# g_final broadcast by TensorE at each tile's end, and two V rows per tile given to VectorE

## What is computed

```python
def peer_ffn(h, w_q, sub_keys, u_tab, v_tab):        # per block of 128 tokens
    q = (hb @ w_q).reshape(PEER_BLOCK, PEER_HEADS, 2, PEER_KEY_DIM // 2)
    ...                                               # top 16 of 128 x 128 keys for each of 8 heads
    gate = jax.nn.softmax(top_s, axis=-1).astype(hb.dtype)
    act = jax.nn.gelu(jnp.einsum('thkd,td->thk', u_tab[e], hb), approximate=False)
    return jnp.einsum('thk,thkd->td', gate * act, v_tab[e])
...
    xp = xp + peer_ffn(rmsnorm(xp, g_ffn[l]), ...)
y_prompt = rmsnorm(xp, g_final)[:, N_META:]
y_sample = rmsnorm(xs, g_final)
```

## Time and profile before

| | us |
|---|---|
| median of 3 runs | 3367.15 |
| span of the profiled execution | 3372.4 |
| TensorE busy | 2967.9 |
| VectorE busy | 2247.2 |
| ScalarE busy | 1569.5 |
| POOL busy | 1299.0 |

### The profile page before, as it was taken

The page is one execution under the profiler, slowest core; times in us unless marked ns, Lnnn a source line. Parts: engine busy times, 40 slices in busy tenths (PEclk is TensorE's granted clock), DMA queues, the critical chain, the costliest instruction groups (busy, mean ns, idle before and its releaser), DMA issues.

```text
span 3372.4 us, 34890 instructions
## 1 busy us (share of the span) xinstructions
PE 2967.9 (88%) x10654; PEld 1563.0 (46%) x10654; DVE 2247.2 (67%) x5353; ACT 1569.5 (47%) x4312; POOL 1299.0 (39%) x1097
## 2 busy tenths in 40 slices
PE   7988899988999898989898888998897988798877
PEld 5764556653445444554454333443353434353322
DVE  1268737685678647884779568866777486873854
ACT  2137334555456334643456345644563454432433
POOL 0023324344344434443434444453334443343532
PEclk8998999999999999999999999999999998899999
DMA  4279999999999999999999999999999989999998
GB/s 175 91 298 362 387 386 396 418 394 421 421 420 411 421 422 419 393 405 422 421 400 413 421 422 421 410 421 422 396 382 408 422 351 333 353 393 369 421 422 342
DMA packets 241250, 1298.74 MB, mean 385 GB/s; under 512 B 46068, under 2 KB 70804, under 8 KB 100646
## 3 DMA queue, kind: packets, MB, share of 16 engines
q0 software_dynamic: 156672, 1140.92, 82.5%
q1 hardware_dynamic: 84390, 155.59, 12.4%
HBM read 1279.41 MB, written 16.44 MB: 384 GB/s over the span
## 4 chain that ended last, share of the span: by engine, by line
PE 44%; DMA 28%; DVE 20%; ACT 4%; issue 2%; SPq 1%; POOL 0%; DVEq 0%; ACTq 0%
PE PS L1096 21%; DMA R<-in_t_uv,idx 18%; DVE R L1746 8%; PE PS L779 7%; DMA R<-in_t_uv,idxS 4%; DMA wring<-in_w_out 3%; PE PS L745 2%; PE PS L1018 2%; PE PS L860 2%; PE PS L859 2%; DVE xb L1757 2%; DMA wring<-in_w_query 2%; PE PS L1045 2%; DVE SC L1712 1%; DVE SC L1709 1%
## 5 line engine op out<-in xcount | busy, mean ns | idle before, releaser
L1096 PE MATMUL PS<-R,diag 128*128 128x512 f32 x3776 | 1821.4, 619 | 200.3 <-ACT diag L1378 173.6
L710 POOL DMA_INDIRECT R<-in_t_uv,idx x1024 | 1234.3, 1205 | 1949.1 <-PE PS L1096 1389.3
L1746 DVE CUSTOM_DVE_ANT_0 R<-R,hb 128x1024 f32<-128x1024 f32 x1088 | 1315.7, 1220 | 726.4 <-DMA R<-in_t_uv,idx 645.3
L1096 PEld LDWEIGHTS PS<-R,diag 128*128 128x128 f32 x3776 | 694.6, 195 | 1077.5 <-issue 635.4
L1369 ACT ACTIVATE acts<-dots 128x1 f32<-128x1 f32 x1088 | 217.2, 200 | 1103.1 <-DVE dots L1746 1100.4
L1378 ACT ACTIVATE diag<-ident,wv 128x128 f32<-128x128 f32 x880 | 353.7, 402 | 76.9 <-PE PS L1096 49.0
L779 PE MATMUL PS<-R 128*128 128x128 f32 (+2 forms) x2272 | 317.1, 295 | 38.6 <-ACT stg L1140 26.7
L779 PEld LDWEIGHTS PS<-R 128*128 128x128 f32 x2272 | 298.5, 196 | 113.1 <-issue 104.5
L1371 ACT ACTIVATE wv<-gate,acts 128x1 f32<-128x1 f32 x1024 | 301.9, 295 | 33.3
L1757 DVE SCALAR_TENSOR_TENSOR xb<-R,wv,xb 128x1024 f32<-128x1024 f32 x144 | 184.4, 1281 | 1.7 <-ACT wv L1371 1.7
L1018 PE MATMUL PS<-wring,T 128*128 128x512 f32 x256 | 133.0, 649 | 42.6 <-DMA wring<-in_w_out 42.6
(11 more groups left out here) (243 smaller groups left out, 2376.0 us busy)
## 6 DMA issues: line engine op xcount, KB each, us to landing
wring<-in_w_out SPq DMA_DIRECT2D x64, 512.0 KB, 14.0
wring<-in_w_query SPq DMA_DIRECT2D x64, 512.0 KB, 8.1
R<-in_t_win SPq DMA_DIRECT2D x38, 512.0 KB, 8.5
R<-in_t_uv,idx POOLq DMA_INDIRECT x1024, 14.0
R<-in_t_win SPq DMA_DIRECT2D x9, 1024.0 KB, 16.0
pr<-prd SPq DMA_DIRECT2D x8, 976.0 KB, 12.7
prd<-stg SPq DMA_DIRECT2D x54, 128.0 KB, 7.6
xb<-in_x_prompt SPq DMA_DIRECT2D x8, 512.0 KB, 7.9
```

The costliest lines, as they stand in the source:

```text
L710: e.indirect_dma_start(dst, None, table, bass.IndirectOffsetOnAxis(ap=index, axis=0)).then_inc(S[s], c.count(name, s, 16))
L1096: m = mm(bank(n), diag[:, NTH[s] % DR, :], pair(s)[:, D + 512 * n:D + 512 * n + 512], start=begins, stop=s == last_slot(t), skip_group_che ...
L1746: e.tensor_tensor_reduce(u, u, hb[:, tile_of(g) % 2, :], 1.0, 0.0, ALU.mult, ALU.add, dots[:, g % NW:g % NW + 1]).then_inc(dve_done, c.cou ...
```

## The change

g_final is no longer loaded per tile. Its two halves are loaded once at the start into free rows of krg (gfin_half), which becomes 1152 wide while PP becomes 1040 wide. In the turn of ysum TensorE waits for ysum and spreads g_final over the 128 partitions with two matmuls of ones (1x128) by a half (1x512) into banks 0 and 1; y then reads Y in place of gfin, after a wait for these matmuls. Since y reads the banks, the first V row that TensorE sums for the next tile waits for y, not for ysum. on_dve also gives VectorE slots 0 and 1 of tiles 2 to 8, so that TensorE's first V row there is that of slot 2, which it reaches in the turn of y. In tile 9 it is still slot 0.

```diff
--- before.py
+++ after.py
@@ -80,7 +80,7 @@
 
 
 def on_dve(s):
-    return s < P * NTILE and 3 <= s % P < 57 and s % P % 3 == 2
+    return s < P * NTILE and (3 <= s % P < 57 and s % P % 3 == 2 or s >= P and s % P < 2)
 
 
 BY_PE = [s for s in range(NSLOT) if not on_dve(s)]
@@ -208,14 +208,14 @@
         epsc = sb("epsc", [P, 2])
 
         ckvT = sb("ckvT", [P, NKEY])
-        krg = sb("krg", [P, NKEY])
+        krg = sb("krg", [P, 1152])
         ckvR = sb("ckvR", [P, (NTILE + 1) * P])
         state = sb("state", [P, 4, 64])
 
         pr = sb("pr", [P, IN_W])
         T1 = sb("T1", [P, D])
         B1 = sb("B1", [P, D])
-        PP = sb("PP", [P, 1152])
+        PP = sb("PP", [P, NKEY])
         scr = sb("scr", [P, 1152])
         ckvS = sb("ckvS", [P, KV])
         krS = sb("krS", [P, ROPE])
@@ -272,7 +272,6 @@
         mask = mask16[:].bitcast(BF16)
 
         held = wring[:, 0:2, :].rearrange("p a d -> p (a d)")
-        gfin = wring[:, 2, :]
         sst = R[:, SAUX:SAUX + 2, :].rearrange("p a (b c e) -> p (a b) c e", b=4, c=4)
         cachev = [R[:, SAUX + 2, :], R[:, SAUX + 3, :]]
         kcT = R[:, SAUX + 4, :]
@@ -282,6 +281,9 @@
         latS = R[:, SAUX + 6, 512:1024]
         pgt = stg[0:1, 0, 0:DEC_B * PAGES].bitcast(I32)
 
+        def gfin_half(n):
+            return krg[32 * n + 32:32 * n + 33, 640:1152]
+
         def gffn_half(n):
             return krg[32 * n + 32:32 * n + 33, 0:512]
 
@@ -378,7 +380,7 @@
             ["w0", "w1", "w2", "w3", "px0", "px1", "px2"] + [f"wc{i}" for i in range(NWC)] + ["ps0", "ps1", "ps2", "ps3", "pr", "prb", "pr0st",
              "xb0", "xb1",
              "trg0", "trg1", "ld_id", "early", "const", "ld_w", "kv_out", "ckvr", "y0", "y1", "st_in", "st_out", "late",
-             "pg", "cv0", "cv1", "gfin"]
+             "pg", "cv0", "cv1"]
         S = {n: ctx.enter_context(nc.semaphore(n + "_done" if n in ("dve", "act", "pe", "pool") else n)) for n in names}
         dve_done, act_done, pe_done, pool_done = S["dve"], S["act"], S["pe"], S["pool"]
 
@@ -464,6 +466,8 @@
             dma(iota[:], A["c_iota"], "const", "iota")
             for n in range(2):
                 dma(gffn_half(n), A["g_ffn"][:, 512 * n:512 * n + 512], "const", f"gffn{n}")
+            for n in range(2):
+                dma(gfin_half(n), A["g_final"].rearrange("(o n) -> o n", o=1)[:, 512 * n:512 * n + 512], "const", f"gfin{n}")
             dma(keysT[:], A["t_keys"], "const", "all")
 
             def prep(p, nj):
@@ -625,8 +629,6 @@
                     e.wait_ge(pe_done, c.at("pe", "meta su"))
                 else:
                     e.wait_ge(pe_done, c.at("pe", f"used q{t - 1}_{NCH - 1}"))
-                if m == 2 and t > 2:
-                    e.wait_ge(dve_done, c.at("dve", f"y{t - 2}"))
                 w = A["w_out" if which == "o" else "w_query"].rearrange("o k n -> (o k) n")
                 k = m % NCH
                 dma(w_buf(t, m), w[k * P:(k + 1) * P, :], f"w{m % nb}", f"{which}{t}_{k}")
@@ -660,9 +662,6 @@
                 for m in range(NCH + nb, 2 * NCH):
                     yield from p.to(1 + m - nb - NCH)
                     load_w(t, m, p)
-                yield from p.to(8)
-                e.wait_ge(pe_done, c.at("pe", f"used q{t}_6"))
-                dma(gfin, A["g_final"].partition_broadcast(P), "gfin", f"g{t}")
 
             def peer(g):
                 for t in range(1, SMP + 1):
@@ -1082,13 +1081,22 @@
                 m.then_inc(pe_done, c.count(f"sc1_{j}"))
 
             def peer(g):
+                for t in range(1, SMP + 1):
+                    if g == last_slot(t) + LAG + 1:
+                        e.wait_ge(dve_done, c.at("dve", f"ysum{t}"))
+                        if t == 1:
+                            e.wait_ge(pool_done, c.at("pool", "ones1"))
+                            e.wait_ge(S["const"], c.at("const", "all"))
+                        for n in range(2):
+                            m = mm(bank(n), ones(n), gfin_half(n), start=True, stop=True)
+                        m.then_inc(pe_done, c.count(f"gfin{t}"))
                 s = g - LAG
                 if not 0 <= s < NSLOT or on_dve(s):
                     return
                 t = tile_of(s)
-                begins = s == P * (t - 1)
+                begins = s == next(x for x in BY_PE if tile_of(x) == t)
                 if begins and t > 1:
-                    e.wait_ge(dve_done, c.at("dve", f"ysum{t - 1}"))
+                    e.wait_ge(dve_done, c.at("dve", f"y{t - 1}"))
                 if s == 0:
                     e.wait_ge(act_done, c.at("act", f"P0_{len(ITEMS[0]) - 1}"))
                 e.wait_ge(act_done, c.at("act", f"d{s}"))
@@ -1736,9 +1744,8 @@
                         e.wait_ge(act_done, c.at("act", f"ysq{t}"))
                         invert(peerv[:, 1:2])
                         settle()
-                        if t < SMP:
-                            e.wait_ge(S["gfin"], c.at("gfin", f"g{t + 1}"))
-                        stt(xb[:, t % 2, :], xb[:, t % 2, :], peerv[:, 1:2], gfin, ALU.mult, ALU.mult).then_inc(
+                        e.wait_ge(pe_done, c.at("pe", f"gfin{t}"))
+                        stt(xb[:, t % 2, :], xb[:, t % 2, :], peerv[:, 1:2], Y, ALU.mult, ALU.mult).then_inc(
                             dve_done, c.count(f"y{t}"))
                 if g < NSLOT:
                     e.wait_ge(S[f"uv{home(g)}"], c.at(f"uv{home(g)}", f"u{g}"))
```

## The result

The changed kernel takes 3395.3 us (median of 5 runs, 3383.37 to 3402.59) where the kernel before, in 5 runs beside it, takes 3368.29: a ratio of 1.0074, 95% interval 1.0051 to 1.0097. That is 17 to 33 us slower. (Every ratio here is estimated from all runs of a kernel and of before beside it, and differs a little from the quotient of the two medians, which is 1.0080 here. A ratio is turned into microseconds by before's time.) The prediction said 4 us, and its range ended at 3381. The profiled execution of after has a span of 3400.8 us, 28.4 more than before's.

What follows compares the result with a forecast made beforehand. DMA was taken to bound second halves of tiles, TensorE the stretches behind tile ends. Loads -7.4 plus 11 of 13.8 us of delay gave +3.6, say +4, on 3367.15: 3371 us, range 3358 to 3381.

Steps and rivals of the forecast that it cites:

- Loads, -7.4: Eight g_final loads go; six, in DMA-bound stretches, come off the time at 1.24 us each: -7.4 us.
- Scores end when they did: At tile ends the broadcast pair, 1.9 us warm, takes the first V row's place and the scores behind end as before.
- The moved rows: At the end of tile 3 VectorE idles 3.58 us before the masked maximum, so its two new rows (2.4 us) are hidden.
- Slots 2 and 3: Waiting for y at the ends of tiles 1, 3, 4 and 6, they end 3.1, 1.9, 4.1 and 2.7 us later: 11.8.
- The cushion at ends 2 and 5: At the ends of tiles 2 and 5, delays of 2 to 2.5 us each go into a cushion: 0.5 us together.
- End of tile 7, 1.5: Slot 2 and the scores come some 3 to 4 us later; the early refill of slot 1's pair gives 2.5 back: 1.5.
- End of tile 8, nothing: Slot 1024 waits for y, some 5 us after ysum; a cushion of 7 us takes the delay: nothing.
- Four fifths paid: Of the 13.8 us of delay at the tile ends, four fifths, 11 us, become time.
- B: VectorE reaches y later than worked out; every end pays fully at the low clock: +13 us, 3380; chance 0.26.
- C: At tile ends VectorE's moved rows don't start before y, which comes 2 us later still: 3382; chance 0.06, in B's tail.

Runs made afterwards that it cites:

- e2: Kernel before plus VectorE taking slots 0 and 1 of tiles 2 to 8 and TensorE's first V row waiting for y; g_final still loaded, no broadcast: 1.0045 of before.
- e4: The whole change, with two full matmuls (4 passes) on TensorE ahead of the broadcast pair at each tile's end: 1.0055 of before.
- e5: As e2, but at the end of tile 7 TensorE waits for ysum as before instead of y: 1.0051 of before.
- e6: The whole change, with three full matmuls into an unused bank between the scores and the wait for y at ends 1 to 6: 1.0045 of before.
- e11: The whole change, with the broadcast pair behind the scores at the ends of tiles 1 to 6, y left in place: 1.0023 of before.
- e8: As e1, but TensorE's first V row of tile 8 alone waits for y, those of tiles 2 to 7 for ysum: 1.0033 of before.
- e7: The whole change, with y one turn earlier on VectorE: 1.0005 of before.
- e10: The whole change, with y one turn earlier on VectorE and the broadcast pair behind the scores at the ends of tiles 1 to 6: 1.0009 of before.
- e12: The whole change, with the pair behind the scores except at ends 3 and 7, and y one turn earlier except at end 4: 3371.37 us, 0.9992 of before.
- e9: Kernel before without the loads of g_final and the two waits that belong to them, everything else the same: 0.9978 of before.
- e1: Kernel before with the exchange of rows alone: VectorE takes slots 0 and 1 of tiles 2 to 8; g_final still loaded, first V row waits for ysum: 1.0002.

## Why the prediction was wrong

Two steps failed above all: that the scores end when they did, and with them y at ends 3, 5 and 6, and the 1.5 us for the end of tile 7. The price is a sum of lateness at the ends. In the table of ends after's sum is 33.6 us above before's; less 7.4 for the loads that is 26, and 25 were measured. That this fits so well is in part luck: 2.3 us of it are the later cache page at end 7, and for other kernels the sum is a rough guide only. It gives 27 for e2 (15 measured), 23 for e4 (19), 21 for e5 (17), 20 for e6 (15), 16 for e11 (8), 4 for e8 (11), -5 for e7 (+2), -7 for e10 (+3), -6 for e12 (-3).

- *Loads, -7.4.* Right, size included (e9).
- *Scores end when they did.* Wrong, and the step on which most of the loss beyond the parts hangs (e11). I took the pair at 1.9 us and warm, in the first V row's place. It takes 1.13 to 2.08 us; the trace of before had it already, since the four passes of g_ffn take 1.13 us together at each of their nine places. Behind it the scores run at the low clock at ends 2, 4, 5 and 6 (e4's full pair undoes that); at end 4 this isn't so in every execution, as e6 and e7 have them at 1.12 us a pair there. At end 5 they end 10.6 us behind ysum, before 9.1. The masked maximum waits for them and y for the maximum: y starts 12.1 us behind ysum at end 5 and 14.0 at end 6, before 10.5 and 12.2. I had it unchanged at ends 3, 5 and 6, and 1.6 later at end 4, where it came 2.1 later. The moved rows themselves are hidden at ends 3, 5 and 6, as said.
- *Slots 2 and 3.* I took 4.7 us at end 3 and 5.2 at end 4, with slot 3 warm again. They took 5.40 and 6.20, at end 5 6.68. Slot 3's lateness at ends 1, 3, 4 and 6 came to 2.0, 4.1, 5.6 and 5.2 us, together 16.9 against 11.8.
- *The cushion at ends 2 and 5.* 3.7 and 5.7 us of lateness, and 0.5 forecast as paid. The place of each dot against before shows both: over the first 32 slots of tiles 3 and 6 after loses 3.7 and 5.7 us, over the rest it wins 3.7 and 4.7. A load's 1.24 us is in each rest, so 2.5 and 3.5 us came back from the cushion, and 1.2 and 2.2 us were paid, 3.4 against 0.5.
- *End of tile 7, 1.5.* The largest miss. I saw that y came late there and priced slot 2 and the scores at 3 to 4 us. That part was right: behind the cache page they came 4.1 us later, and the other 2.3 of the 6.4 us are the page itself. What was wrong is what it costs. I let the early pair of slot 1 give 2.5 us back, and nothing of that can be seen: tile 8 takes 410.5 us from its first dot to the next tile's where it took 396.8, and e8 measured 10.4 us (by its ratio over e1's; 2 to 19 by both intervals). Against the exchange alone the scores are 6.9 us late behind the page, since the exchange had brought them 2.9 us forward. Why 4 to 7 us at the scores become 11 to 15 over the tile isn't shown.
- *End of tile 8, nothing.* Right: from the first to the 33rd slot of tile 9 after loses 0.7 us.
- *Four fifths paid.* Too low, as far as one trace each can tell. Behind ends 1, 3, 4 and 6 after loses 2.1, 3.5, 4.1 and 8.5 us over the first 32 slots, together 18.2 where slot 3's lateness was 16.9. In tile 7 after's dots are 5.2 us later at slot 4, still 5.2 at slot 16, and 8.5 at slot 32.

Of the rivals B was nearest: the wait for y decides at every end but the last, and it named the sample steps' chain at tile 7. But it had the scores on time too, so even its +13 fell short. C did not occur: both moved rows start ahead of y, 2.3 and 4.6 us behind ysum at ends 1 to 7.

What stays open: the share of the clock (e4, e6), and where in tile 8 the price of end 7 falls. At the dot of slot 6 the six kernels with the wait stand 38 to 41 us behind the tile's first dot and the others 25 to 34, but further on single executions differ by some 7 us (before has a hole of that length at slots 92 to 96 that e1 lacks, and e7 and e10 lose as much by slot 32).

## What to carry to other kernels

When an operand moves into a buffer that the next stage needs, the reader of that operand becomes the release of the buffer: look for what stands ahead of that reader on its engine, and move it forward first (here one turn, 23 us). Price the parts together too: pair and wait cost little and 14.5 us alone, and some 30 together. A short operation in the place of a long one ahead of work at the low clock need not make that work earlier by the difference: here the scores behind the long one ran at 1.12 to 1.47 us a pair and behind the short one at 2.07. And a wait that is cheap at the regular ends can be dear at the one end where another chain runs through the same engines, so each end is priced by itself.

## What the runs showed of the hardware

The broadcast pair takes less time than its passes added up. All passes of it in after:

```profile
L1091 PE MATMUL PS<-krg x36: 587/692/1218, 621.8 to 3393.6; 1*128 1x512 f32 x36
```

Four passes of 692 ns (median) take 1.13 us together, and 2.08 at the low clock, a little over half of the 1.98 to 3.78 of a V row's four. The two halves of g_final lie in different rows (partitions 32 and 64), and in e10 a pass of a score of 32 rows, from 1367.42 to 1367.70, runs inside the pair's first two, from 1367.20 to 1367.90 (lines above; the starts are recorded, the ends of matmuls are modelled). The Trainium skill (TensorEngine Tiling (Array Packing), section Key Properties) says that different tiles of the array can do weight loads and matmuls in parallel. The rows agree with that, but that it is the cause isn't shown: no run places both halves in the same rows. In after the pair ran at 1.13 us behind idle times of 1.3 to 3.3 us (six ends), at 1.68 behind 2.6 us (end 2) and at 2.08 behind 4.9 and 5.6 us. The idle time just ahead doesn't say it all: in e10 the pair of end 5 took 2.08 us behind 1.1 us.
